# Operand tiles and weight slots at other distances in SBUF

## The reference, cut to what matters

```python
def hybrid_layer(x, pos, st, wl):
    h = rmsnorm(x, g_mix)
    z = h @ w_in                       # 2048 -> 11 * 512 columns
    ...                                # four mixers: conv module, short conv, RG-LRU, retention
    mix = jnp.concatenate([y_a, y_b, y_c, y_d], axis=-1)
    x = x + mix @ w_out                # 2048 -> 2048
    h2 = rmsnorm(x, g_ffn)
    gpre, new_conv_ffn = causal_dwconv(h2 @ w_ffn_gate, conv_ffn, w_conv_ffn)
    x = x + (jax.nn.silu(gpre) * (h2 @ w_ffn_up)) @ w_ffn_down   # 2048 -> 5632 -> 2048
```

## Time and profile before

| | |
|---|---|
| median of 3 runs | 2444.77 us (2442.79 to 2444.85) |
| the profiled execution | 2442.28 us, of which the span from first to last instruction is 2440.5 us |
| PE busy | 2343.5 us, 96% |
| PEld busy | 2321.7 us, 95% |
| DVE busy | 1713.6 us, 70% |
| ACT busy | 1004.5 us, 41% |
| mean granted TensorE clock | 0.977 of full speed |
| DMA | 424 MB, 174 GB/s mean |

### The profile page before, as it was taken

One profiled execution on the slowest core, in us unless ns is written; L12 is line 12 of the kernel. 1 busy time (PEld: TensorE's weight loads), 2 busy tenths in 40 slices (PEclk: granted clock), 3 DMA queues, 4 the chain that ended last, 5 costly groups with the idle time before them and its releaser, 6 DMA issues.

```text
span 2440.5 us, 48608 instructions
## 1 busy us (share of the span) xinstructions
PE 2343.5 (96%) x18842; PEld 2321.7 (95%) x18842; DVE 1713.6 (70%) x2620; ACT 1004.5 (41%) x1095; POOL 0.2 (0%) x4
## 2 busy tenths in 40 slices
PE   7998989999999999999999988999999999999996
PEld 7997989999999999999998978999999999999995
DVE  6894686766666666666669947767666766666666
ACT  5332544434434444434443326344443443444433
POOL 0000000000000000000000000000000000000000
PEclk9998999999999999999999989999999999999998
DMA  7553455555555555555464534555555555555552
GB/s 249 169 162 128 156 160 180 182 182 181 181 179 182 182 180 180 183 179 181 161 196 158 168 125 144 175 185 181 182 180 180 180 181 181 180 180 180 180 181 97
DMA packets 118824, 424.22 MB, mean 174 GB/s; under 512 B 15457, under 2 KB 15713, under 8 KB 118753
## 3 DMA queue, kind: packets, MB, share of 16 engines
q1 hardware_dynamic: 111312, 405.80, 50.9%
q10 hardware_dynamic: 7440, 17.44, 2.0%
HBM read 413.71 MB, written 9.48 MB: 173 GB/s over the span
## 4 chain that ended last, share of the span: by engine, by line
PE 87%; DVE 8%; DVEq 2%; ACT 1%; issue 1%; DMA 0%; ACTq 0%
PE bank L475 28%; PE bank L476 28%; PE bank L477 28%; DVE wl L708 3%; DVE av L689 2%; PE bank L584 1%; PE bank L577 1%; ACT wh L192 1%; DVEq L690 1%; DVEq L861 1%; DVE q L907 1%; DVE xl L702 0%; PE bank L595 0%; PE bank L612 0%; DVEq L966 0%
## 5 line engine op out<-in xcount | busy, mean ns | idle before, releaser
L475 PE MATMUL bank<-xh,wh 128*128 128x264 f32 x4224 | 1217.0, 288 | 50.3 <-DVE wl L708 30.6
L708 DVE TENSOR_TENSOR wl<-raw,wh 128x1024 fp32r<-128x1024 f32 x768 | 938.6, 1223 | 439.7 <-ACT wh L422 224.0
L476 PE MATMUL bank<-xl,wh 128*128 128x264 f32 x4224 | 1208.9, 286 | 0.0
L477 PE MATMUL bank<-xh,wl 128*128 128x264 f32 x4224 | 1207.8, 286 | 0.0
L475 PEld LDWEIGHTS bank<-xh,wh 128*128 128x128 f32 x4224 | 808.6, 191 | 59.5 <-DVE wl L708 32.3
L422 ACT ACTIVATE wh<-raw 128x1024 fp32r<-128x1024 f32 x480 | 509.5, 1062 | 828.5 <-PE bank L477 828.5
L476 PEld LDWEIGHTS bank<-xl,wh 128*128 128x128 f32 x4224 | 809.2, 192 | 0.4
L477 PEld LDWEIGHTS bank<-xh,wl 128*128 128x128 f32 x4224 | 804.4, 190 | 0.0
L192 ACT ACTIVATE wh<-raw 128x1024 fp32r<-128x1024 f32 x288 | 302.7, 1059 | 466.3 <-PE bank L477 455.7
L475 PE MATMUL bank<-hh,wh 128*128 128x264 f32 x1408 | 399.4, 284 | 7.2 <-DVE hl L1034 6.6
L477 PE MATMUL bank<-hh,wl 128*128 128x264 f32 x1408 | 401.1, 285 | 0.0
(11 more groups left out here) (189 smaller groups left out, 1057.9 us busy)
## 6 DMA issues: line engine op xcount, KB each, us to landing
raw<-in_weights SPq DMA_DIRECT2D x768, 512.0 KB, 3.4
x<-in_x_in SPq DMA_DIRECT2D x4, 528.0 KB, 6.6
out_y<-x ACTq DMA_DIRECT2D x4, 528.0 KB, 2.6
s_own<-in_ret_state ACTq DMA_DIRECT2D x4, 512.0 KB, 4.7
k<-in_ret_state ACTq DMA_DIRECT2D x4, 512.0 KB, 4.9
out_new_ret_sample<-s_own ACTq DMA_DIRECT2D x4, 512.0 KB, 4.0
out_new_ret_sample<-k ACTq DMA_DIRECT2D x4, 512.0 KB, 2.8
dg<-in_ffn_state ACTq DMA_DIRECT2D x2, 528.0 KB, 6.1
```

Source lines behind the costliest of these rows:

```text
L475: pe.matmul(out, w_hi, rh, start=first, stop=False)
L476: pe.matmul(out, w_hi, rl, start=False, stop=False)
L477: return pe.matmul(out, w_lo, rh, start=False, stop=last)
L708: tt(wl[:, i, :], raw[:, i, :], wh[:, i, :].bitcast(F32), ALU.subtract).then_inc(lo_made, 1)
```

## The change

Operands and weight slots are allocated wider than they are used, and only the used part is addressed. A tile of the normalised input then lies 1152 bytes behind the one before (288 floats), one of the mixers' output 1280 (320), one of the hidden block 1088 (272), and a slot of `raw`, `wh` or `wl` 4224 (1056). A tile of 128 bytes, never used, is allocated ahead of all others. The area reserved for descriptors of dynamic DMAs is 1024 bytes on a partition; without the argument it is 16384. No instruction is added or removed, and the work and its order stay.

```diff
+X_STRIDE, M_STRIDE, H_STRIDE, W_STRIDE = 288, 320, 272, CHUNK + 32
...
+        def operand(name, tiles, stride, used):
+
+            return sb(name, [P, tiles, stride], F32R)[:, :, 0:used]
+
+        sb("lead", [P, 32])
         x = sb("x", [P, KT, T])
-        xh, xl = sb("xh", [P, KT, T], F32R), sb("xl", [P, KT, T], F32R)
-        mh, ml = sb("mh", [P, KT, T], F32R), sb("ml", [P, KT, T], F32R)
-        hh, hl = sb("hh", [P, 4, T], F32R), sb("hl", [P, 4, T], F32R)
-        raw = sb("raw", [P, RING, CHUNK])
-        wh, wl = sb("wh", [P, RING, CHUNK], F32R), sb("wl", [P, RING, CHUNK], F32R)
+        xh, xl = operand("xh", KT, X_STRIDE, T), operand("xl", KT, X_STRIDE, T)
+        mh, ml = operand("mh", KT, M_STRIDE, T), operand("ml", KT, M_STRIDE, T)
+        hh, hl = operand("hh", 4, H_STRIDE, T), operand("hl", 4, H_STRIDE, T)
+        raw = sb("raw", [P, RING, W_STRIDE])[:, :, 0:CHUNK]
+        wh, wl = operand("wh", RING, W_STRIDE, CHUNK), operand("wl", RING, W_STRIDE, CHUNK)
...
-    nc = bacc.Bacc("TRN2", target_bir_lowering=False, num_devices=1)
+    nc = bacc.Bacc("TRN2", target_bir_lowering=False, num_devices=1, dynamic_dma_scratch_size=1024)
```

## The result

The changed kernel takes 2457.01 us (median of 5 runs, 2456.68 to 2457.85) against 2444.85 us for the kernel before beside it: ratio 1.0049, 95% interval 1.0035 to 1.0064. It is slower by 12 us, where 25 us of gain were forecast. Its profiled execution has a span of 2454.9 us, 14.4 more than before. The granted clock is the same (0.976 against 0.977), the instructions are the same, and so is all that is not TensorE.

The account below looks back on a forecast made before the run. TensorE's matmul spacing was taken as the bound: 27.0 us (input, mixer output) plus 2.1 (hidden tile), 29.1, times 0.856 gives 25; 2442.3 less 25 is 2417.3, plus 2.5 for the median: 2420 us. The 8-in-10 range was 2365 to 2475.

Parts of the forecast that it names:

- TensorE's spacing bounds the kernel, and the layout acts on it alone: In the MLP stretches TensorE is 100% busy, limited by the distance between matmul starts, 120.9 ns.
- descriptor area, lead and four-run copies cost nothing: Smaller descriptor area, 128-byte lead, and copies into the padded mixer operand as four runs of 264: no cost taken.
- Some 11 ns neither columns nor load: On each of 18,432 streamed matmuls, some 11 ns beyond columns and load, 199 us in all, inferred to depend on addresses.
- the load's 109 ns: Weight load of 128x128 and matmul of 128 plain fp32 columns follow each other in 109 ns, taken as the floor.
- the value of the tiles that stand now where all will stand: Input and mixer output would take 118.9 ns a matmul, as k-tiles 0 and 4 now, against 120.8: 27.0 us.
- Meets in a worse place: Rival: a fixed phase between moving tile and weights is bad at every matmul; 39 us lost, 2484 us; chance 0.25.
- The spacing does not move: Rival: the matmul spacing stays at 120.9 ns whatever the padding, time at 2444 us; chance 0.18.
- Faster still: Rival: drift itself costs, so the fastest threes (0.35, 116.7 ns) become the rule; 66 us gained, 2379 us; chance 0.20.
- The two small terms: Mixer output's 1,536 matmuls at 118.9 ns, within the 27.0 us; hidden tile's 4,224 gaining 0.5 ns each, 2.1 us.
- What share reaches the end, 0.856: Matmuls in the fully busy stretches count whole, the other 5,442 half: 0.856 of 29.1 us, 25 us.

Follow-up runs that it names:

- run 1: Kernel before with only the 128-byte lead tile and smaller descriptor area, all tile and slot distances as before; ratio 0.9998.
- run 4: Kernel before with 21 lines of 48 loads and matmuls added behind its end, varying places, columns and distances; not timed beside it, 320 columns 146.7 ns.
- run 6: Kernel before with 64 lines of 48 over pairs of places and ten column-count lines added behind its end; not timed beside it, spacing 120.0 to 126.7 ns.
- run 5: Kernel before with all operand tiles 1280 bytes apart, slots at 4096, descriptor area 1024 bytes, no lead; ratio 1.0002.
- run 9: Kernel before with the same 48 matmuls after 14 preludes, and 15 distance lines, added behind its end; not timed beside it, 120 or 121.2 to 121.5 ns.
- run 12: Kernel before with all operand tiles 1280 bytes apart and the input's low part 32 bytes further on the grid; 2427.2 us, ratio 0.9932.

## Why the prediction was wrong, step by step

- **TensorE's spacing bounds the kernel, and the layout acts on it alone.** Right: splits, loads and waits kept their numbers, and the 12 us are in the distance between matmuls. That descriptor area, lead and four-run copies cost nothing was right too (run 1; 1088 ns against 1089).
- **"Some 11 ns neither columns nor load".** Right as a number, wrong in what I made of it. I looked for it in addresses, with up to 199 us at stake. Runs 4 and 6 show 10 to 17 ns behind the columns from 256 to 512 of them at full clock, and none at the 1.2 GHz level (220 ns for 264). Over 63 pairs of places the spacing moves from 120.0 to 126.7 ns, and no address takes it lower., from which I took the load's 109 ns, are transposes through TensorE (L534), which the prediction calls matmuls; for float32r the like came out, 110.6 ns at 128 columns.
- **The failing step: "the value of the tiles that stand now where all will stand", 118.9 ns from k-tiles 0 and 4.** A matmul's spacing is not a property of its own place. Repeated alone, the place of k-tile 4 takes 123.5 ns (run 4); the fastest pair takes 121.5 (run 6); one layout takes 119.9 or 121.3 (run 5); identical matmuls in one line take 115 to 126 (run 9). Picking two of eight k-tiles out of a periodic pattern picked halves of its swing. The only sum that could be read was the whole period, 2.90 us, and it says nothing of another layout. Input chunks came out at 2.92 and 2.94 (+15.8 us by 528 chunks) instead of 2.854 (24 x 118.9 ns): 122.1 ns a matmul, not 118.9. The runs show in its place a spacing that the whole sequence of matmuls settles, and that what ran before can settle otherwise.
- **The rivals.** "Meets in a worse place", 0.25 and 2484 us, had the sign. Its price was again a single three (0.37), 39 us against the 12 measured, and its mechanism, a fixed phase that is bad at every matmul, is not borne out: threes on one place took 0.35 to 0.38 us after the change, and run 12, with one place for every tile but those of `xl`, is the fastest. "The spacing does not move" fell, by 0.9 ns in the first stretch. "Faster still" fell: 116.7 ns is nowhere a steady rhythm.
- **The two small terms.** The mixers' output, forecast at 118.9 ns, came out at 122.1 in the first layer and 120.1 in the second. The hidden block gained some 0.25 ns where 0.5 was forecast. That is luck: it rests on the same step, and the low part `hl` stood 128 bytes off the place of `hh` in the kernel before (4 x 1056 = 16.5 x 256), which the working leaves out.
- **What share reaches the end, 0.856.** Not contradicted: 13.6 us by it for the input, 12 measured in all. The two are too rough to test it more closely.

What stays open is what TensorE carries from one matmul to the next, why the extra is there at 2.4 GHz alone, and why 32 bytes between high and low part lead into the short rhythm: the runs show the rhythms, not where they come from.

## What to carry to other kernels

A spacing that swings with a fixed pattern is to be read over its whole period; single members of the pattern are not prices that a new layout can choose from. Before a layout is changed to help matmuls, some lines of them behind the end of the kernel, in its own order and over the distances in question, sort out the candidates in one profile. They are no forecast: the distance of 1280 bytes read 120.0 ns in the lines, and the kernel with it (run 5) gained nothing, because a layout may have several steady rhythms. So the same lines should be read after more than one prelude, and a wide spread between runs of one kernel is a reason to compare stretches within its trace. A second small offset may then pick a rhythm, as the 32 bytes did here.

## What the runs showed of the hardware

- With a load of 128x128 float32r weights before each, a float32r matmul of 320 to 512 columns takes its columns at 2.4 GHz and 13 to 14 ns more (146.7 ns at 320, 227.5 at 512, run 4). Between 256 and 296 columns the extra is 10 to 17 ns and uneven: 280 columns take longer than 288 (133.3 and 131.7 ns, run 6). At 128 to 240 columns the spacing stays at 110.6 to 112.3 ns.
- At a granted clock of 0.50 the same pairs with 264 columns start 220 ns apart: the columns at 1.2 GHz without an extra (run 4).
- 48 identical pairs of load and matmul settle at 120 or at 121.2 to 121.5 ns by the seven that went before them (run 9), and such a rhythm lasts for 600 us and more (119.9 or 121.3 ns, run 5).
